# Attention written out as one pipeline of 64 rows per layer, with scores two rows ahead and in front of a row's transposes

## The reference

```python
for l in range(DEPTH):                      # 2
    z = rms_norm(x, norm1_gain[l]) @ w_in[l]        # q | k | v | u, 512 columns each
    q, k = rope(rms_norm(q per head)) * 64**-0.5, rope(rms_norm(k per head))
    # 8 heads of 64; causal windows (128, 1), (512, 4), (2048, 16), merged by their softmax sums
    att = dilated_attention(q, k, v)
    pool = pool_mixer(u, w_pool[l], pool_scale[l])
    x = x + concat(att, pool) @ w_out[l]
    x = x + hier_moe(rms_norm(x, norm2_gain[l]), ...)
```

## Time and profile before

| | |
|---|---|
| median of 3 runs | 1797.02 us (1796.76 to 1799.8) |
| profiled execution, its own time | 1796.23 us |
| its span | 1794.2 us, 23296 instructions |
| PE busy | 1496.5 us, 83% |
| DVE busy | 831.2 us, 46% |
| ACT busy | 485.1 us, 27% |
| attention of layer 0 | 247.81 to 424.51, 176.70 us |
| attention of layer 1 | 1119.83 to 1297.41, 177.58 us |
| DMA | 228.11 MB, mean 127 GB/s |

### The profile page before, as it was taken

How to read it: one execution, slowest core, us unless ns; L and a number is a source line. 1 busy time by engine, 2 the same in 40 slices (tenths; PEclk the granted TensorE clock), 3 DMA queues, 4 the chain that set the end, 5 groups by cost and what they waited for, 6 DMA issues and landing times.

```text
span 1794.2 us, 23296 instructions
## 1 busy us (share of the span) xinstructions
PE 1496.5 (83%) x6931; PEld 1073.7 (60%) x6932; DVE 831.2 (46%) x2101; ACT 485.1 (27%) x916; POOL 272.3 (15%) x259
## 2 busy tenths in 40 slices
PE   3999977888993999998269998888899749999960
PEld 2887866777882444444158786777768624444430
DVE  3777666565436122211377766665543442222114
ACT  3222156663211011111212212566611201111000
POOL 1200058002001011110300001920200021111114
PEclk8999989999996999999589999899999869999985
DMA  8400020000047588942640002000000845888637
GB/s 302 164 29 0 0 95 1 0 0 0 36 147 263 163 294 299 368 158 88 245 161 0 1 0 94 1 0 0 0 12 35 295 138 172 296 301 293 225 123 287
DMA packets 118473, 228.11 MB, mean 127 GB/s; under 512 B 6184, under 2 KB 72816, under 8 KB 118416
## 3 DMA queue, kind: packets, MB, share of 16 engines
q1 hardware_dynamic: 90352, 129.55, 21.1%
q0 software_dynamic: 18128, 65.71, 10.3%
q10 hardware_dynamic: 9936, 32.14, 4.4%
HBM read 183.33 MB, written 44.04 MB: 127 GB/s over the span
## 4 chain that ended last, share of the span: by engine, by line
PE 71%; DVE 10%; issue 8%; ACT 5%; DMA 4%; ACTq 1%; POOL 0%; DVEq 0%; PEld 0%; POOLq 0%; SPq 0%; PEldq 0%
PE ps L1521 18%; PE ps L1315 17%; PE ps L1448 9%; PE ps L1295 9%; PE ps L1534 8%; PE ps L1408 5%; ACT arena L730 2%; PE ps L1462 2%; DMA arena<-token_rows,next_tok 1%; ACT arena L742 1%; DMA big<-y_table,pos_i 1%; DVE arena L1021 1%; DVE w_in_lo L913 1%; PE ps L1375 1%; PE ps L1377 1%
## 5 line engine op out<-in xcount | busy, mean ns | idle before, releaser
L1295 PE MATMUL ps<-cst,arena 128*128 128x128 f32 x1682 | 247.7, 283 | 145.4 <-DVE arena L884 56.9
L1521 PE MATMUL ps<-big,arena 128*128 x720 | 325.3, 605 | 10.6 <-issue 9.9
L1295 PEld LDWEIGHTS ps<-cst,arena 128*128 128x128 f32 x1682 | 199.1, 145 | 223.2 <-DVE arena L884 59.1
L874 DVE TENSOR_TENSOR arena<-ps,par 128x512 f32<-128x512 f32 x126 | 81.2, 687 | 365.2 <-PE ps L1295 365.2
L1521 PEld LDWEIGHTS ps<-big,arena 128*128 128x128 f32 x720 | 135.5, 193 | 171.5 <-issue 171.5
L1315 PE MATMUL ps<-w_in_hi,hT_hi 128*128 128x512 f32 x512 | 206.8, 404 | 12.6 <-DVE w_in_lo L913 8.6
L1315 PE MATMUL ps<-w_in_lo,hT_hi 128*128 128x512 f32 x512 | 202.2, 395 | 0.0
L1315 PE MATMUL ps<-w_in_hi,hT_lo 128*128 128x512 f32 x512 | 202.2, 395 | 0.0
L1534 PE MATMUL ps<-big,arena 128*128 x360 | 166.6, 607 | 7.0 <-issue 7.0
L1408 PE MATMUL ps<-big,arena 128*128 x1152 | 149.6, 276 | 0.0
L1408 PEld LDWEIGHTS ps<-big,arena 128*128 128x128 f32 x1152 | 144.7, 193 | 5.4
(11 more groups left out here) (159 smaller groups left out, 1764.4 us busy)
## 6 DMA issues: line engine op xcount, KB each, us to landing
big<-in_w_gate SPq DMA_DIRECT2D x32, 1024.0 KB, 8.5
big<-in_w_up SPq DMA_DIRECT2D x32, 1024.0 KB, 11.2
big<-in_w_down SPq DMA_DIRECT2D x32, 1024.0 KB, 13.0
y_table<-arena ACTq DMA_DIRECT2D x45, 512.0 KB, 7.0
big<-in_w_in SPq DMA_DIRECT2D x18, 1024.0 KB, 10.6
big<-in_w_out SPq DMA_DIRECT2D x4, 2048.0 KB, 10.2
token_rows<-arena ACTq DMA_DIRECT2D x16, 512.0 KB, 2.8
y_table<-x_res POOLq DMA_DIRECT2D x15, 512.0 KB, 9.5
```

The lines of the kernel that those rows point to most:

```text
L874: ins = ve.tensor_tensor(out=dst[:, 4 * h:4 * h + 4, :], in0=ps[:, banks + h, :].rearrange("p (a c) -> p a c", c=P), in1=spread(gain[:, 4 ...
L1295: ins = te.transpose(ps[:, bank + i // 4, (i % 4) * P:(i % 4 + 1) * P], src, ident)
L1521: ins = te.matmul(ps[:, 2, :], xgT[:, k, :], big[:, ds(at + k * 2 * FE, 2 * FE)], start=k == 0, stop=k == K - 1)
```

## The change

The loops over pairs are written out: each engine runs rows m = 0 to 63 of a layer, with p = m // 16 and n = m % 16, and the edges between pairs are gone from the row order.

- TensorE: the body of a row becomes scores(m + 2), probs_t(m), probs_v(m - 1). Scores run over pair boundaries. The transposes of `att` become `att_t(p)`, placed after probs_t of row 1 of the next pair. It waits for over_sum(15) of its pair, for the copy of row 17 (bank 4) and for the last `half_evac` (bank 5). probs_t of row 2 waits for both evacuations of `att`.
- ScalarE: exp(m + 1) also runs over boundaries. `att_evac(p - 1)` comes after the copy of row 1 of the next pair, ahead of that row's `k_top`.
- VectorE: mask(m + 2) and over_sum(m - 1) run over boundaries; its chain semaphore is reset once a layer.
- The staging for a pair after the last is left out, and the semaphore targets count it no more (`q_high_in`, `k_high_in` and `staged` have one step less per layer).
- `probs_v` takes its columns of `v` from a constant and not from the loop's register.

The functions below are the core of the diff; the others change only in their counting (m for p and n).

```diff
+ROWS_A = HEADS * T
...
-                with a_.Fori(0, PAIRS) as p:
-                    def exp(n):
...
-                    exp(0)
-                    for n in range(16):
-                        i, b = n % T, n % 2
-                        if n + 1 < 16:
-                            exp(n + 1)
...
-                        if n == 0:
-                            a_.wait_ge(s_done, upto(l, 16 * PAIRS, p * 16))
-                            q_top(p, 1)
-                        if n == 8:
-                            a_.wait_ge(s_done, upto(l, 16 * PAIRS, p * 16 + 8))
-                            q_top((p + 1) % PAIRS, 0)
-                        if n == 1:
-                            k_top(p, 1)
-                        if n == 9:
-                            k_top((p + 1) % PAIRS, 0)
-                        if n == 2:
-                            k_top_again(p, 1)
-                        if n == 10:
-                            k_top_again((p + 1) % PAIRS, 0)
...
+                def exp(m):
+                    i, b = m % T, m % 2
+                    nk = (i + 1) * P
+                    a_.wait_ge(sm_ready, upto(l, ROWS_A, m + 1))
+                    sc.activation(pr[b][:, 0:nk], pr[b][:, 0:nk], ACT.Exp, scale=-1.0,
+                                  bias=st[:, 64 + m % 16:65 + m % 16],
+                                  accum_out=st[:, 80 + m % 16:81 + m % 16]).then_inc(p_ready, 1)
+                def att_evac(p):
                     for h in range(2):
                         a_.wait_ge(at_done, upto(l, 2 * PAIRS, p * 2 + h + 1))
                         sc.activation(attT[:, p, h * 512:(h + 1) * 512], ps[:, 4 + h, :], ACT.Copy).then_inc(at_ev, 1)
+                exp(0)
+                for m in range(ROWS_A):
+                    p, n, i, b = m // 16, m % 16, m % T, m % 2
+                    if m + 1 < ROWS_A:
+                        exp(m + 1)
+                    nb = min(i + 1, 4)
+                    a_.wait_ge(pt0_done, upto(l, ROWS_A, m + 1))
+                    if m >= 2:
+                        a_.wait_ge(pv_done, upto(l, ROWS_A, m - 1))
+                    sc.activation(prT[b][:, 0:nb, :], ps[:, 4, 0:nb * P]
+                                  .rearrange("p (a c) -> p a c", c=P), ACT.Copy).then_inc(pt0_ev, 1)
+                    if p and n == 1:
+                        att_evac(p - 1)
+                    if n == 0:
+                        a_.wait_ge(s_done, upto(l, ROWS_A, p * 16))
+                        q_top(p, 1)
+                    if n == 1:
+                        k_top(p, 1)
+                    if n == 2:
+                        k_top_again(p, 1)
+                    if p < PAIRS - 1:
+                        if n == 8:
+                            a_.wait_ge(s_done, upto(l, ROWS_A, p * 16 + 8))
+                            q_top(p + 1, 0)
+                        if n == 9:
+                            k_top(p + 1, 0)
+                        if n == 10:
+                            k_top_again(p + 1, 0)
+                att_evac(PAIRS - 1)
...
-                with dve.Fori(0, PAIRS) as p:
-                    ch.restart()
...
-                    mask(0)
-                    mask(1)
-                    for n in range(16):
-                        if n % T >= 4:
-                            half_evac(n)
-                        if n + 2 < 16:
-                            mask(n + 2)
-                        if n >= 1:
-                            over_sum(n - 1)
-                        if n == 3:
-                            q_and_k_low(p, 1, 2 * p + 1)
-                        if n == 11:
-                            q_and_k_low((p + 1) % PAIRS, 0, 2 * p + 2)
-                    over_sum(15)
...
+                def mask(m):
+                    n, i, b = m % 16, m % T, m % 2
+                    nk = (i + 1) * P
+                    if m >= 2:
+                        j = m - 2
+                        if j % T >= 4:
+                            dve.wait_ge(pt1_done, upto(l, 8 * PAIRS, 4 * (j // T) + j % T - 3))
+                        else:
+                            dve.wait_ge(pt0_done, upto(l, ROWS_A, j + 1))
+                    dve.wait_ge(s_done, upto(l, ROWS_A, m + 1))
...
+                    dve.wait_ge(at_done, upto(l, 2 * PAIRS, m // 16 * 2))
...
+                ch.restart()
+                mask(0)
+                mask(1)
+                for m in range(ROWS_A):
+                    p, n = m // 16, m % 16
+                    if m % T >= 4:
+                        half_evac(m)
+                    if m + 2 < ROWS_A:
+                        mask(m + 2)
+                    if m >= 1:
+                        over_sum(m - 1)
+                    if n == 3:
+                        q_and_k_low(p, 1, 2 * p + 1)
+                    if n == 11 and p < PAIRS - 1:
+                        q_and_k_low(p + 1, 0, 2 * p + 2)
+                over_sum(ROWS_A - 1)
...
+                def scores(m):
+                    a, i, b = m // T % 2, m % T, m % 2
                     if i == 0:
-                        pe.wait_ge(staged, upto(l, 2 * PAIRS + 1, p * 2 + a + 1))
-                    if n >= 2:
-                        pe.wait_ge(sm_ready, upto(l, 16 * PAIRS, p * 16 + n - 1))
+                        pe.wait_ge(staged, upto(l, 2 * PAIRS, m // T + 1))
+                    if m >= 2:
+                        pe.wait_ge(sm_ready, upto(l, ROWS_A, m - 1))
...
-                pe.wait_ge(sm_ready, upto(l, 16 * PAIRS, 0))
-                scores(0, 0)
-                scores(0, 1)
-                with pe.Fori(0, PAIRS) as p:
-                    pe.wait_ge(at_ev, upto(l, 2 * PAIRS, p * 2))
...
-                    for n in range(16):
-                        probs_t(n)
-                        if n + 2 < 16:
-                            scores(p, n + 2)
-                        if n >= 1:
-                            probs_v(n - 1)
-                    probs_v(15)
-                    with pe.If(p < PAIRS - 1):
-                        pe.wait_ge(sm_ready, upto(l, 16 * PAIRS, p * 16 + 16))
-                        scores(p + 1, 0)
-                        scores(p + 1, 1)
-                    pe.wait_ge(o_ev, upto(l, 16 * PAIRS, p * 16 + 16))
...
+                def probs_t(m):
+                    i, b = m % T, m % 2
+                    pe.wait_ge(p_ready, upto(l, ROWS_A, m + 1))
+                    pe.wait_ge(pt0_ev, upto(l, ROWS_A, m))
+                    blocks = cols(pr[b], i + 1)
+                    transposes(4, blocks[0:4]).then_inc(pt0_done, 1)
+                    if i >= 4:
+                        pe.wait_ge(pt1_ev, upto(l, 8 * PAIRS, m // T * 4 + i - 4))
+                        transposes(5, blocks[4:]).then_inc(pt1_done, 1)
+                def probs_v(m):
+                    p, i, b = m // 16, m % T, m % 2
+                    pe.wait_ge(pt0_ev, upto(l, ROWS_A, m + 1))
+                    if i >= 4:
+                        pe.wait_ge(pt1_ev, upto(l, 8 * PAIRS, m // T * 4 + i - 3))
+                    if m >= 2:
+                        pe.wait_ge(o_ev, upto(l, ROWS_A, m - 1))
+                    for j in range(i + 1):
+                        ins = te.matmul(ps[:, 6 + b, 0:P], prT[b][:, j, :], v[:, j, p * P:(p + 1) * P],
+                                        start=j == 0, stop=j == i)
+                    ins.then_inc(pv_done, 1)
+                def att_t(p):
+                    pe.wait_ge(o_ev, upto(l, ROWS_A, 16 * p + 16))
+                    pe.wait_ge(pt0_ev, upto(l, ROWS_A, min(16 * p + 18, ROWS_A)))
+                    pe.wait_ge(pt1_ev, upto(l, 8 * PAIRS, 8 * p + 8))
                     for h in range(2):
                         transposes(4 + h, [att[:, 4 * h + i, :] for i in range(4)]).then_inc(at_done, 1)
+                scores(0)
+                scores(1)
+                for m in range(ROWS_A):
+                    if m + 2 < ROWS_A:
+                        scores(m + 2)
+                    if m >= 18 and m % 16 == 2:
+                        pe.wait_ge(at_ev, upto(l, 2 * PAIRS, m // 16 * 2))
+                    probs_t(m)
+                    if m >= 16 and m % 16 == 1:
+                        att_t(m // 16 - 1)
+                    if m >= 1:
+                        probs_v(m - 1)
+                probs_v(ROWS_A - 1)
+                att_t(PAIRS - 1)
```

87 lines of the change are left out of this document (21 added, 66 removed).

## The result

The changed kernel takes 1771.0 us (median of runs from 1770.73 to 1774.17). The kernel before took 1797.99 in the same comparison. The ratio is 0.9853 with a 95% interval of 0.9836 to 0.987: faster by about 26.5 us. The forecast was 1758.8, so about 70% of the predicted gain of 38.2 us came. The profiled execution took 1771.18 us with a span of 1769.1, so 25.1 us of span went where 38.2 were forecast.

A forecast was written before the change was run, and what follows sets the result against it. TensorE bounds the kernel, losing time in waits between pairs and inside heads. Seams 32.4, first halves 1.6 and last halves 4.2 sum to 38.2 us off 1796.2: 1758.0, as run median 1758.8, range 1748 to 1771.

The forecast's parts named there:

- I take the same loss, plus or minus 2 us: First two pairs: `k_low` stretched to 2.82 us beside GpSimd while TensorE idles; loss kept unchanged, plus or minus 2 us.
- The Exp chain leaves 0.2 idle: 4.6: Rows 12 and 13: TensorE's own work 4.4 us plus 0.2 idle, 4.6 against 5.86 in the old order.
- Its own 0.9 us of transposes hidden behind ScalarE's backlog: First half of a next pair: the `att` transposes add no time; only 0.7 us of idle before them counts.
- The evacuations at 1.2 us: First half of a next pair: two `att` evacuations on ScalarE, ahead of `k_top`, add 2 x 0.59 = 1.2 us.
- First half of the first pair, 0.8 a layer: Layer's start: scores(2) need only mask(0) and masks come earlier, gaining 0.8 us a layer, 1.6 in all.
- the last half: Last pair's second half: staging for a nonexistent pair goes, 18.7 against 20.8 us, gaining 2.1 a layer.
- no stall from the longer code: Code written out four times loads more instructions; about 1 us a packet, none of it taken as exposed.
- Less: the seam's thin rows run dry: Rival, 17%: a seam costs 1 us more and its halves gain nothing from reordering, another 1 us; 1771.
- Its argument from the clock: Support for the smaller-gain rival: granted clock 0.96 in the pair whose first rows idle, 1.00 in the next.
- More: Rival, 15%: earlier masks also shorten ScalarE-bound rows, a pair nears 36.2 us, 12 us more gain; 1747.
- Slower: Rival, 3%: written-out code adds 57 packets, each exposed for 1 us, giving 1816.
- no change: Rival, 2%: only the 2.64 us idle goes, `att` backlog takes most back; 4 us gained, 1792, or less.

The follow-up runs named there:

- with pieces: Kernel before and changed kernel, each with all long GpSimd instructions beside attention cut in pieces of 256 and 512 columns: 1790.41 and 1761.33 us.
- split_q: Changed kernel with VectorE's `q_and_k_low` cut in two, its q part one row earlier in the code: 1761.4 us, ratio 0.9809.
- tiny_evac: Changed kernel with both `att` evacuations writing one column in the first three pairs: 1787.7 us, a total that says nothing since values change; only rows count.
- swap_only: Kernel before, loop over pairs kept, with scores(n + 2) ahead of the transposes of row n: 1792.03 us, ratio 0.9975.
- unroll_only: Changed kernel, written out, but with the old order inside a row (transposes before scores): 1773.92 us, ratio 0.9878.
- after_pieces: Changed kernel with all long GpSimd instructions cut in pieces and nothing else: 1761.33 us, ratio 0.98.
- all_pieces: Changed kernel with `q_and_k_low` cut, its q part earlier, and every long GpSimd instruction in pieces: 1745.78 us, ratio 0.971.
- mid_pool_cut: Changed kernel with GpSimd's two-input instructions in pieces, ScalarE staging one row later, VectorE's q after row 3 and k after row 4: 1758.85 us.
- stage_late: Changed kernel with ScalarE staging two rows later and VectorE's two parts behind rows 3 and 4: 1773.2 us, ratio 0.9875.

## Why the forecast missed, step by step

The mechanism was right in direction and place: the drain between pairs goes, and most of the gain stands there. The step that failed is the sum, in three of its terms: the loss beside GpSimd, rows 12 and 13, and the first half of a layer. All three came out dearer than the prediction had them.

1. **"I take the same loss, plus or minus 2 us"** (GpSimd beside `k_low`) failed. The two first seams lost 9.8 us against clean ones before and 14.2 after, 4.4 more. The prediction treated the loss as a stretch of one instruction that moves along. The runs show a hold that ends 1.08 to 1.09 us after the GpSimd instruction does, whatever VectorE's arrival. In layer 0 TensorE's first wait ends at 282.98 after and at 282.71 before, since GpSimd's instruction there ends at nearly the same time in both (281.64 and 281.38). Row 16 then starts 5.15 us earlier than before (291.0 against 296.15), but the second wait ends only 2.03 earlier (307.08 against 309.11): VectorE arrives early and meets the instruction of 8.97 us, where before it met one of 3.21. The first seams gained 2.31 and 1.87, and with pieces 3.6 each. The Trainium skill, "SBUF — State Buffer", section "SBUF: two separate sides", says that a VectorE instruction with two SBUF inputs and a GpSimd instruction that reads SBUF lock each other out for a whole instruction. The traces agree, with 8.43 us in split_q for an instruction of 1.22. The earlier trace rows showed the stretched instruction alone; the end of the GpSimd instruction beside it, 281.38 against 282.46, would have shown a hold and not a slowdown.
2. **"The Exp chain leaves 0.2 idle: 4.6"**, for rows 12 and 13, failed: 5.26, and 5.50 for rows 20 and 21 of the half with `att`. That is 0.66 and 0.90, 1.56 a seam. The limit is VectorE's chain: mask(13), two staging instructions, mask(14). It starts with mask(13), which I took to come about 1 us earlier; it comes 0.61 earlier, because its releaser is now transposes(11), which at the packed price of 0.109 a block would be over in 0.44 us but complete after 0.63, with 0.29 more to the mask. The rest was too short in the working itself: 5.86 less 1 is 4.9 and not 4.6. split_q shows the chain: with one staging instruction taken out of it the rows take 4.42 and 4.40.
3. **"Its own 0.9 us of transposes hidden behind ScalarE's backlog"** failed: they stand in the open in row 17 (+1.58 with the 0.52 of idle). **The evacuations at 1.2 us** were too dear; tiny_evac shows about 0.5. The errors cancel by luck: rows 16 to 19 cost 2.12 us more for `att` where the terms gave 2.1. The sum was right, its parts were not.
4. **First half of the first pair, 0.8 a layer**, failed: -0.2 and 0.0. Scores(2) now stand ahead of transposes(0), at the lower clock level (granted 0.50 from 247 to 252 us). From the first score matmul to transposes(0) it takes 2.38 us (248.09 to 250.47), before 1.88 (247.81 to 249.69). By row 8, 0.3 of this has come back (18.96 us from transposes(0) on, before 19.23). The order alone does this: up to row 8, swap_only takes 21.35 us in both layers and unroll_only, with the old order, 21.14 and 21.12. So the new order costs 0.2 us here. The kernel before has 21.11 and 21.35; in its layer 1 the granted clock was still 0.50 from 1123 to 1127 us, where in layer 0 it was 0.69 from 251 to 255.

In a clean seam item 2 costs 1.56 us and item 3 nothing. Rows 8 to 11 (7.83 and not 8.0) and smaller parts gave 0.4 back. That leaves 1.2 between 37.9 forecast and 39.1 measured. The table's 4.2 for four clean seams is a little less than four times that, since it goes by a gain of 5.4 where 43.36 - 37.9 is 5.46, and since one seam before took 43.69. The two first seams hold another 2.3 of it, so 4.3 of their 6.6 stand beside GpSimd. Of these the pieces gave back 3.1. The rest, 0.65 a seam, lies beside GpSimd's pieces, mostly in the half with `att` (21.53 us in after_pieces, 20.72 in a clean seam); which instruction passes it on was not tried.

**Right as forecast**: rows 8 to 12 (7.83 against 8.0), 14 and 15 (2.37 and 2.90 against 2.3 and 2.9), the last half (2.08 against 2.1, though 0.7 of it is the order and not the staging to which the term was put down), two table loads, no clock loss in a clean pair (1.00; the first seam of layer 1 had some), and no stall from the longer code. That last is a bound: there are 24 more instruction packets, and the stretches of attention account for the whole gain (25.55 against 25.1 us).

**The rivals.** "Less: the seam's thin rows run dry" gave 1771, and that is the number, but not quite its mechanism: it put 1 us on dry thin rows and 1 on halves without gain from the order. The thin rows do stand dry by 0.52, the order does give 0.9 a pair, and a large piece came from GpSimd, which the rival does not mention. That its number fits is luck. Its argument from the clock carries no time: the pair granted 0.96 took 43.36 us and the next, at 1.00, 43.33. "More" put a pair at 36.2; split_q and all_pieces reached 37.13 in a clean one, so 2 us of slack were there, behind VectorE's chain. ScalarE's copies hold less: rows 8 to 11 fell by 0.3 in mid_pool_cut and 0.5 in stage_late. "Slower" and "no change" did not come.

## What to carry to other kernels

When work is moved ahead on one engine, look at what then becomes the last releaser of each buffer on the others, and price it with a row of completion, not with the packed rate. A stretched instruction beside a long one on another engine may be a hold with a fixed end: then earlier arrival brings nothing, and cutting the long instruction does. Removing a drain between loop passes pays, here 3.4 us of 4.3 a seam, and a finer order pays only as far as the slowest chain allows: moving one 1.22 us instruction by a row brought 9.6 us in the changed kernel and nothing measurable in the kernel before, where the hold took back half of what the rows gained.
